# Delta rule: the 8-wide diagonal blocks of a triangular inverse solved on VectorE, in place of two levels of products on TensorE

## The chip, the cores and the metric

The kernel runs on one core of a Trainium2 chip. The metric is device time in microseconds (us). "Before" was timed three times, and its profile is of one further execution.

## The reference

One decoder layer over 256 tokens of width 2048: an input projection, two token mixers (a gated delta rule and a differential softmax attention), a gated merge, an output projection with a layer norm, and a SwiGLU feed-forward with a layer norm. The part that matters is the delta rule, for 16 heads in chunks of 64 tokens:

```
a_mat = where(strict, einsum(k_beta, k) * decay, 0)          # 64 x 64, strictly lower triangular
u, w  = triangular_solve(a_mat + eye(64), [v * beta, k_beta * exp(g)])
then, chunk after chunk:  v_new = u - w S ;  o = q_dec S + qk v_new ;  S = S * g_tot + k_tail^T v_new
```

All of it is float32.

## The kernel before

**Large products.** Every weight matrix is cut into tiles of 256 rows by 512 columns. SP loads a tile into one of four buffers of `raw`; ScalarE rounds it into `whi` (L836, by `split`), VectorE subtracts to get the rest `wlo` (L1416, by `split`), and TensorE multiplies with both, 12 matmuls a tile (`gemm_tile`, L477, all recorded at L458). `split(n, s)` in slot s prepares tile s + 3. A body is 32 tiles, so it has 32 slots; in each slot every engine does its share of the tile and then the small work that the slot is given. The order is written by hand: each engine runs its own stream, and semaphores join them.

**The delta rule between the tiles.** Four heads and their four chunks of 64 are handled in each of the first four bodies (NB = 4); body 0 has a stream of its own, on VectorE and ScalarE bodies 1 to 3 are one loop. `dn_build(j, s)` builds the inverse of `a_mat + eye` in slots 13 to 27. Each 64 x 64 matrix is first treated as two diagonal blocks of 32, which lie as 8 groups of 32 columns on 128 partitions (128 x 256 elements in all). Slot 15 on VectorE makes the masked blocks `WT` (four operations, one for each 32 partitions) and the starting inverse `TT` for blocks of 2. Then five levels, slots 17 to 21 (`GROW`): TensorE multiplies (32 matmuls of 32 x 32 blocks; L595, recorded at L458, `B<-Pm,Pc`), and VectorE subtracts from PSUM, transposes and masks, and so hands `Pc` to the next level (L1601 to L1613). The first and the last level have 32 columns, the three between have 64. Slots 22 and 23 (`OFF_P`, `OFF_T`) make the 32 x 32 block off the diagonal, ScalarE copies the results in slot 24, and slots 25 and 26 make the part that joins the two halves of the 64-blocks.

On TensorE the products of a slot stand behind the tile of that slot, and wait for the semaphore `dve_x` (`dve_t`, `dve_p` in the later slots; `act_tt` for ScalarE's copies). On VectorE the operations of a slot stand behind its `split`, and most wait for the one before them by a counter (`ch`).

**Other work in the same slots.** VectorE: `MASK` (slots 17, 18) masks `decm`; `O_LO` (19, 20) splits an output of the body before; the convolution (`CONV_SLOTS`, L1560) has six passes in each of slots 22, 23, 29 and 30 and a transpose in 21 and 28. ScalarE: `silu(j, 1)` stands behind its copies in slot 24.

Of the kernel before, what the change touches and what calls it, by code (L numbers as in the profile page):

```python
# [18 lines left out]
ALU = mybir.AluOpType  # L19
# [3 lines left out]
P = 128  # L23
# [7 lines left out]
CH = 64  # L31
# [10 lines left out]
PV_SLOTS = [10, 15, 20, 25]  # L42
OH_SLOTS = [14, 19, 24, 29]
OA_SLOT, OA_HI, OA_LO, OA_LAST = 0, 8, 11, 29
CONV_LINKS, BUILD_LINKS, SCAN_LINKS, DA_LINKS = 12, 20, 7, 25
OT_SLOTS = (12, 14)
O_SCALED, O_BLOCKS, V_BLOCKS = 11, 12, 25
O_HI, O_LO = 18, (19, 20)
MASK = (17, 18)
SCAN = 1  # L50
TURN = range(1, 7)
# [4 lines left out]
DECAY = range(5, 9)  # L56
WARM = 2
LATE_LO = 4
GROW = {17: 0, 18: 1, 19: 2, 20: 3, 21: 4}
GROWN = len(GROW)  # L60
OFF_P, OFF_T = 22, 23
TPG = KC // TK
RING = 4
AHEAD = 3
# [39 lines left out]
def build(nc, xT, xrow, weights, w_ab, consts, early, params, lam_in, ln_in, out):  # L104
# [8 lines left out]
    with ctx:  # L113
# [81 lines left out]
        B8 = [b[:, :].rearrange("p (h d) -> p h d", h=8) for b in B]  # L195
        C8 = [b[:, 0:8 * SB].rearrange("p (h d) -> p h d", h=8) for b in B]
        TT, WT = Pm[:, :, 0:SB], Pm[:, :, SB:CH]

        def conv_in(kind, h):

# [86 lines left out]
        def end_at(s):  # L287
# [28 lines left out]
            dve_lnT dve_x1 pe_x1T x1f act_x1T dve_x1T pe_y act_beta act_gc pe_gT act_gT act_var dve_var act_root act_sig act_xn pro_chain ln_chain""".split()  # L316

        counted = """pe_conv dve_raw dve_conv act_silu dve_cw act_tap
            dve_g act_past act_decay pe_ktok act_sqk dve_ktail pe_kk dve_at dve_t act_tt dve_x pe_x pe_p dve_p pe_t
            pe_p21 act_p21 pe_x21 act_x21 dve_vS dve_v pe_kq dve_qk  # L320
            pe_z dve_vn pe_so act_s act_o0 pe_ks dve_r pe_o1 dve_o1 pe_qtok act_osq act_sqq
            dve_oh dve_oS pe_oT act_oT dve_oT
# [133 lines left out]
        def _(pe):  # L456
# [112 lines left out]
            def dn_build(j, s):  # L569

                if s == 13:
                    pe.wait_ge(N["act_silu"], 1 + 3 * j + 1)
                    pe.wait_ge(N["dve_conv"], 1 + 6 * j + 2)
                    pe.wait_ge(N["act_sqq"], 1 + j)
                    for t in range(TOK):
                        for h in range(HB):
                            last = nc.tensor.transpose(B4[3 - 2 * t][:, h, :], cT[:, 0, h, t * P:(t + 1) * P], ident)  # L577
                    last.then_inc(N["pe_ktok"], 1)
                if s == 14:
                    pe.wait_ge(N["act_sqk"], 1 + 2 * j + 2)  # L580
                    pe.wait_ge(N["dve_ktail"], 1 + j + 1)
                    for t in range(TOK):
                        for h in range(HB):
                            kc = cT[:, 0, h, t * P:(t + 1) * P]
                            last = mm(B4[2 + t][:, h, :], kc, kc)
                    last.then_inc(N["pe_kk"], 1)
                if s in GROW:
                    k = GROW[s]
                    f0, f1 = SB if k == 0 else 0, SB if k == GROWN - 1 else CH
                    pe.wait_ge(N["dve_x"], 1 + GROWN * j + k + 1)  # L590
                    waits_end()
                    for i in range(8):
                        for q in range(4):
                            a = sub(q)
                            last = mm(B8[1][a, i, f0:f1], Pc[a, i, :], Pm[a, i, f0:f1])  # L595
                    last.then_inc(N["pe_x"], 1)
                if s == OFF_P:
                    pe.wait_ge(N["dve_t"], 1 + 2 * j + 1)
                    waits_end()
                    for i in range(8):  # L600
                        for q in (0, 2):
                            last = mm(C8[2][sub(q + 1), i, :], AT[sub(q), i, sub(q + 1)], Tc[sub(q), i, :])
                    last.then_inc(N["pe_p"], 1)
                if s == OFF_T:
                    pe.wait_ge(N["dve_p"], 1 + j + 1)
                    waits_end()
                    for i in range(8):
                        for q in (0, 2):
                            b = sub(q + 1)
                            last = mm(C8[1][sub(q), i, :], Pc[b, i, :], TT[b, i, :])  # L610
                    last.then_inc(N["pe_t"], 1)
                if s == 25:
                    pe.wait_ge(N["dve_t"], 1 + 2 * (j + 1))
                    pe.wait_ge(N["act_tt"], 1 + j + 1)
                    waits_end()
                    for i in range(HB):
                        mm(B8[1][CH:P, i, :], AT[0:CH, i, CH:P], T[0:CH, i, :])
                        last = mm(B8[1][0:CH, HB + i, :], AT[0:CH, HB + i, CH:P], T[0:CH, HB + i, :])
                    last.then_inc(N["pe_p21"], 1)
                if s == 26:  # L620
                    pe.wait_ge(N["act_p21"], 1 + j + 1)
                    waits_end()
                    for i in range(HB):
                        mm(B8[2][0:CH, i, :], Pm[CH:P, i, :], TTf[CH:P, i, CH:P])
                        last = mm(B8[1][0:CH, i, :], Pm[0:CH, HB + i, :], Pm[0:CH, i, :])
                    last.then_inc(N["pe_x21"], 1)
# [207 lines left out]
        def _(act):  # L834
# [157 lines left out]
            def dn_build(j, s):  # L992
# [17 lines left out]
                if s == 14 and isinstance(j, int):  # L1010
                    decay(j)
                if s == 24:
                    act.wait_ge(N["dve_t"], 1 + 2 * j + 1)
                    for q in range(4):
                        a = slice(q * SB, (q + 1) * SB)
# [2 lines left out]
                        a = slice(q * SB, (q + 1) * SB)  # L1018
                        last = copy(T[a, :, a], Tc[a])
                    last.then_inc(N["act_tt"], 1)  # L1020
                    silu(j, 1)
                if s == 25:
                    act.wait_ge(N["dve_t"], 1 + 2 * (j + 1))
                    act.wait_ge(N["act_tt"], 1 + j + 1)
                    copy(Pm[0:CH, 0:HB, :], TTf[CH:P, HB:8, CH:P])
                    act.wait_ge(N["pe_p21"], 1 + j + 1)
                    copy(Pm[CH:P, 0:HB, :], B8[1][CH:P, 0:HB, :])
                    copy(Pm[0:CH, HB:8, :], B8[1][0:CH, HB:8, :]).then_inc(N["act_p21"], 1)
                if s == 26:
                    act.wait_ge(N["pe_x21"], 1 + j + 1)  # L1030
                    copy(TTf[0:CH, 0:HB, CH:P], B8[2][0:CH, 0:HB, :], -1.0)
                    copy(TTf[0:CH, HB:8, CH:P], B8[1][0:CH, 0:HB, :], -1.0).then_inc(N["act_x21"], 1)
# [379 lines left out]
        def _(dve):  # L1412
# [56 lines left out]
            def prologue(s):  # L1469
# [9 lines left out]
                if s == 11:  # L1479
                    m0, e0, i0 = (CONST[n][0] for n in ("pairs", "eye", "incl"))  # L1480
                    levels = cst[:, m0:m0 + 6 * CH].rearrange("p (m c) -> p m c", c=CH)
                    for q in range(4):
                        a, f = slice(q * SB, (q + 1) * SB), q % 2 * SB
                        V.tensor_copy(masks[a, 0, :], levels[a, 0, f:f + SB])
                        V.tensor_copy(masks[a, 2:6, :], levels[a, 2:6, f:f + SB])
                        V.tensor_copy(masks[a, 6, :], cst[a, e0 + f:e0 + f + SB])
                        tt(masks[a, 1, :], cst[a, i0 + f:i0 + f + SB], cst[a, e0 + f:e0 + f + SB], ALU.subtract)
                if s == 4:
                    a0 = CONST["negdist"][0]
                    pro(ts(c("same"), cst[:, a0:a0 + P], -1e9, ALU.is_ge))  # L1490
# [80 lines left out]
            def dn_build(j, s, ch):  # L1571
# [16 lines left out]
                if s == 15:  # L1588
# [6 lines left out]
                        a = slice(q * SB, (q + 1) * SB)  # L1595
                        last = tt(WT[a], AT[a, :, a], rep(masks[:, 1, :], 8)[a], ALU.mult)
                    ch(last)
                    ch(tt(Tc[:, :, :], WT, rep(masks[:, 0, :], 8), ALU.mult))
                    V.transpose(flat(Pc[:, :, :]), flat(Tc[:, :, :])).then_inc(N["dve_x"], 1)
                    ch(tt(TT, rep(masks[:, 6, :], 8), Tc[:, :, :], ALU.subtract))  # L1600
                if s in GROW:  # L1601
                    k = GROW[s]
                    dve.wait_ge(N["pe_x"], 1 + GROWN * j + k + 1)
# [2 lines left out]
                        V.transpose(Tc[:, :, :], TT).then_inc(N["dve_t"], 1)  # L1606
                    else:
                        if k == 0:
                            ch(tt(WT, WT, B8[1][:, :, SB:CH], ALU.subtract))
                        else:  # L1610
                            ch(tt(Pm[:, :, :], Pm[:, :, :], B8[1], ALU.subtract))
                        ch(V.transpose(Tc[:, :, :], WT))
                        tt(Pc[:, :, :], Tc[:, :, :], rep(masks[:, k + 2, :], 8), ALU.mult).then_inc(N["dve_x"], 1)  # L1613
                if s in MASK:
                    i = MASK.index(s)
                    ch(tt(decm[:, 4 * i:4 * i + 4, :], decm[:, 4 * i:4 * i + 4, :], rep(c("same"), 4), ALU.mult))
# [589 lines left out]
```

## Time and profile before

| | |
|---|---|
| median of 3 timed runs | 1911.3 us (1910.58 to 1912.15) |
| profiled execution | 1913.78 us |
| its span | 1911.9 us |
| mean granted clock of TensorE | 0.998 of full speed |
| busy, TensorE (matmul) / VectorE / ScalarE | 99% / 69% / 48% of the span |

The span is from the first to the last instruction of the profiled execution; what lies around it is 1.9 us. The profiled execution is 2.5 us above the median of the timed runs. A busy TensorE says here that matmuls follow each other without a gap, and the work between the tiles is part of that.

### The profile page before, as it was taken

What the parts mean: (1) busy time and instruction counts of PE and PEld (TensorE: products, weight loads), DVE (VectorE), ACT (ScalarE), POOL (GpSimd) and SP (SyncE); (2) the same over time, 40 slices, a digit from 0 to 9 for tenths busy, and PEclk for the clock granted to TensorE, in tenths of its full rate; (3) what the DMA queues carried; (4) which work ended last, traced back from release to release, by engine and by line L of the source; (5) the groups of instructions that cost most, each with busy time, mean ns of one, the idle gap of its engine ahead of it and who ended that gap; (6) DMA issues with size and microseconds to landing.
All of it is one profiled execution on the core that took longest, in us unless ns stands there. A gap on an engine that the chain in (4) does not pass through costs nothing.

```text
span 1911.9 us, 31044 instructions
## 1 busy us (share of the span) xinstructions
PE 1896.8 (99%) x10215; PEld 1562.9 (82%) x10215; DVE 1318.8 (69%) x1829; ACT 919.0 (48%) x1270; POOL 189.8 (10%) x424
## 2 busy tenths in 40 slices
PE   9999999999999999999999999999999999999997
PEld 7888887878888888888888887888888888888886
DVE  7869788787766667676577657676774466654657
ACT  5655565554455555456444436444443444433442
POOL 0202021020014151414000000000000000000000
PEclk9999999999999999999999999999999999999999
DMA  7666657475667676766665675555655556555555
GB/s 271 190 208 199 210 188 210 164 222 166 199 202 229 223 236 214 245 212 201 217 195 187 223 252 189 177 195 188 198 194 192 195 190 195 193 195 192 193 189 175
DMA packets 115094, 387.68 MB, mean 203 GB/s; under 512 B 14192, under 2 KB 21168, under 8 KB 114864
## 3 DMA queue, kind: packets, MB, share of 16 engines
q1 hardware_dynamic: 97904, 351.65, 56.0%
q10 hardware_dynamic: 11712, 22.04, 3.7%
q0 software_dynamic: 5376, 12.59, 2.4%
q8 instruction: 68, 1.11, 0.2%
q14 instruction: 34, 0.28, 0.1%
HBM read 367.86 MB, written 18.37 MB: 202 GB/s over the span
## 4 chain that ended last, share of the span: by engine, by line
PE 98%; DVE 1%; issue 0%; ACT 0%; DMA 0%; DVEq 0%; SPq 0%; ACTq 0%
PE pg L458 92%; PE B L458 5%; DVE gates L1424 1%; DMA raw<-in_weights 0%; PE B L558 0%; PE B L577 0%; PE B L671 0%; ACT whi L836 0%; PE B L782 0%; DVE wlo L1416 0%; DVE act_b L1416 0%; PE B L710 0%; DVE lnst L2087 0%; DVE sm L1424 0%; DVE lnst L2092 0%
## 5 line engine op out<-in xcount | busy, mean ns | idle before, releaser
L1416 DVE TENSOR_TENSOR wlo<-raw,whi 128x1024 fp32r<-128x1024 f32 (+1 forms) x640 | 778.6, 1219 | 476.4 <-ACT whi L836 459.2
L836 ACT ACTIVATE whi<-raw 128x1024 fp32r<-128x1024 f32 (+1 forms) x640 | 674.1, 1057 | 766.4 <-PE pg L458 744.9
L458 PE MATMUL pg<-whi,act_x 128*128 128x512 f32 x2960 | 941.8, 394 | 0.6 <-ACT whi L836 0.6
L458 PEld LDWEIGHTS pg<-whi,act_x 128*128 128x128 f32 x2960 | 556.6, 188 | 125.1 <-issue 9.4
L458 PE MATMUL pg<-wlo,act_x 128*128 128x512 f32 x1480 | 574.9, 390 | 1.4 <-issue 1.4
L458 PE MATMUL pg<-whi,act_a 128*128 128x512 f32 x1632 | 504.9, 389 | 0.1
L458 PEld LDWEIGHTS pg<-whi,act_a 128*128 128x128 f32 x1632 | 306.3, 188 | 64.4 <-DVE act_a L1416 0.8
L458 PEld LDWEIGHTS pg<-wlo,act_x 128*128 128x128 f32 x1480 | 278.5, 188 | 54.7
L458 PE MATMUL pg<-wlo,act_a 128*128 128x512 f32 x816 | 317.5, 389 | 0.0
L458 PEld LDWEIGHTS pg<-wlo,act_a 128*128 128x128 f32 x816 | 153.2, 188 | 31.6
L458 PE MATMUL pg<-whi,act_b 128*128 128x512 f32 x512 | 158.4, 389 | 0.0
L458 PEld LDWEIGHTS pg<-whi,act_b 128*128 128x128 f32 x512 | 96.1, 188 | 19.9
L458 PE MATMUL pg<-wlo,act_b 128*128 128x512 f32 x256 | 99.6, 389 | 0.0
L1848 DVE STREAM_TRANSPOSE soft<-hraw 32x256 f32<-32x256 f32 x208 | 90.6, 436 | 3.8
L458 PEld LDWEIGHTS pg<-wlo,act_b 128*128 128x128 f32 x256 | 48.0, 188 | 10.0
L1424 DVE SCALAR_TENSOR_TENSOR cT<-vda,cw,cT 128x255 f32<-128x255 f32 (+2 forms) x96 | 42.0, 479 | 1.3
L1137 ACT ACTIVATE soft<-soft,sm 128x128 f32<-128x128 f32 (+1 forms) x64 | 28.4, 445 | 27.8 <-DVE sm L1420 27.7
L1364 POOL TENSOR_TENSOR half<-dsm 128x8 f32<-128x8 f32 x24 | 13.6, 566 | 257.6 <-DVE dsm L1421 256.3
L1424 DVE SCALAR_TENSOR_TENSOR soft<-cst,sm,B 128x384 f32<-128x384 f32 x32 | 18.2, 611 | 21.0 <-PE B L458 20.3
L1366 POOL TENSOR_SCALAR half<-half 128x2 f32<-128x2 f32 (+1 forms) x72 | 31.3, 435 | 6.3
L1375 POOL DMA_DIRECT2D gates<-turn_p x48 | 26.1, 550 | 37.3 <-DMA turn_p<-gates 37.3
L1375 POOL DMA_DIRECT2D qT<-turn_c x32 | 17.7, 560 | 114.2 <-DMA turn_c<-hraw 114.2
(251 smaller groups left out, 1089.2 us busy)
## 6 DMA issues: line engine op xcount, KB each, us to landing
raw<-in_weights SPq DMA_DIRECT2D x646, 512.0 KB, 4.2
turn_c<-hraw ACTq DMA_DIRECT2D x8, 512.0 KB, 3.6
qT<-turn_c POOLq DMA_DIRECT2D x32, 128.0 KB, 4.7
turn_q<-hraw ACTq DMA_DIRECT2D x6, 512.0 KB, 3.5
gates<-turn_q ACTq DMA_DIRECT2D x24, 128.0 KB, 4.4
turn_p<-gates POOLq DMA_DIRECT2D x12, 192.0 KB, 3.7
gates<-turn_p POOLq DMA_DIRECT2D x48, 48.0 KB, 3.7
decm<-sums_out ACTq DMA_DIRECT2D x4, 512.0 KB, 4.2
```

The source lines that it names most:

```text
L458: return nc.tensor.matmul(o, l, r, start=start, stop=stop)
L836: return nc.scalar.activation(o, i, ACT.Copy, scale=scale)
L1137: last = nc.scalar.activation(pr[:, m, a:b], pr[:, m, a:b], ACT.Exp, bias=sm[:, 28 + i:29 + i], accum_out=sm[:, 32 + i:33 + i])
L1364: ch(G.tensor_tensor(a, o, o, ALU.mult))
L1366: ch(G.tensor_scalar(a, a, -0.5, 1.5, ALU.mult, ALU.add))
L1375: pool.dma_start(dst[b * SB:(b + 1) * SB], scratch[:, :, b].rearrange("a x (q i) -> x a q i", i=SB)).then_inc(full, 16)
L1416: return V.tensor_tensor(o, a, b, op)
L1424: return V.scalar_tensor_tensor(out=o, in0=a, scalar=s, in1=b, op0=op0, op1=op1)
L1848: ins = V.transpose(blocks_out(turned)[b * SB:(b + 1) * SB, :, :, a, :], blocks_in[a * SB:(a + 1) * SB, :, :, b, :])
```

## The change

The two smallest block sizes above 2 are left out of the levels: `GROW` has three entries, in slots 20 to 22. The inverses of the 8 x 8 diagonal blocks now come from forward substitution on VectorE. Slot 16 transposes `WT` with its columns rearranged, multiplies by a selection mask `sel`, adds up, and so lays one 8 x 8 block on each partition (`a8`, 64 elements), beside an identity `t8`. Seven steps follow, each of two operations on `[128, n, k+1]` elements (7 to 16 of them): `u8 = column * row`, `t8 = t8 - u8`. One step is in slot 16, three each in slots 17 and 18. Slot 19 spreads `t8` out again, and two transposes give `TT` and `Tc`, with which the first of the remaining products starts. `OFF_P`, `OFF_T` and the slots of the 64-blocks come one slot later, ScalarE's copies move from slot 24 into 25, behind `silu`, and `O_LO` moves to slots 26 and 27.

```diff
-CONV_LINKS, BUILD_LINKS, SCAN_LINKS, DA_LINKS = 12, 20, 7, 25
+CONV_LINKS, BUILD_LINKS, SCAN_LINKS, DA_LINKS = 12, 33, 7, 25
-O_HI, O_LO = 18, (19, 20)
+O_HI, O_LO = 18, (26, 27)
-GROW = {17: 0, 18: 1, 19: 2, 20: 3, 21: 4}
+GROW = {20: 0, 21: 1, 22: 2}
-OFF_P, OFF_T = 22, 23
+OFF_P, OFF_T, OFF_COPY, OFF_64 = 23, 24, 25, 26
+EB = 8
+SOLVE = {16: range(0, 1), 17: range(1, 4), 18: range(4, 7)}
...
+        sel = masks[:, 0, 0:SB // EB]
+        eye8 = masks[:, 2:4, :].rearrange("p m c -> p (m c)")
+        a8, t8, u8 = (Tc[:, 2 * i:2 * i + 2, :].rearrange("p m c -> p (m c)").rearrange("p (r c) -> p r c", c=EB) for i in range(3))
+        def rows_apart(rows):
+            return rows.rearrange("p i (b g) -> p g i b", g=EB)
+        def blocks_apart(buf):
+            return buf[:, :, :].rearrange("p g (b x) -> p g b x", x=EB)
+        def below(k):
+            n = EB - 1 - k
+            return [ap.broadcast_to([P, n, k + 1]) for ap in (a8[:, k + 1:EB, k:k + 1], t8[:, k:k + 1, 0:k + 1])] + [
+                u8[:, 0:n, 0:k + 1], t8[:, k + 1:EB, 0:k + 1]]
...
# TensorE, dn_build
-                            last = mm(B8[1][a, i, f0:f1], Pc[a, i, :], Pm[a, i, f0:f1])
+                            last = mm(B8[1][a, i, f0:f1], (Tc if k == 0 else Pc)[a, i, :], Pm[a, i, f0:f1])
-                if s == 25:
+                if s == OFF_64:
-                if s == 26:
+                if s == OFF_64 + 1:
...
# ScalarE, dn_build
                 if s == 24:
+                    silu(j, 1)
+                if s == OFF_COPY:
                     act.wait_ge(N["dve_t"], 1 + 2 * j + 1)
...
-                    silu(j, 1)
-                if s == 25:
+                if s == OFF_64:
-                if s == 26:
+                if s == OFF_64 + 1:
...
# VectorE, prologue, slot 11
-                        V.tensor_copy(masks[a, 0, :], levels[a, 0, f:f + SB])
-                        V.tensor_copy(masks[a, 2:6, :], levels[a, 2:6, f:f + SB])
-                        V.tensor_copy(masks[a, 6, :], cst[a, e0 + f:e0 + f + SB])
+                        V.tensor_copy(masks[a, 4:6, :], levels[a, 4:6, f:f + SB])
+                    V.tensor_reduce(sel, ident.rearrange("p (m b) -> p b m", b=SB // EB), X, ALU.add)
+                    pro(V.memset(eye8, 0.0))
+                    pro(V.memset(eye8[:, 0:EB * EB:EB + 1], 1.0))
...
# VectorE, dn_build: slot 15 ends with the first line's wait
                     ch(last)
-                    ch(tt(Tc[:, :, :], WT, rep(masks[:, 0, :], 8), ALU.mult))
-                    V.transpose(flat(Pc[:, :, :]), flat(Tc[:, :, :])).then_inc(N["dve_x"], 1)
-                    ch(tt(TT, rep(masks[:, 6, :], 8), Tc[:, :, :], ALU.subtract))
+                if s == 16:
+                    ch(V.transpose(Tc[:, :, :], rows_apart(WT)))
+                    ch(tt(blocks_apart(Pc), blocks_apart(Tc), sel.unsqueeze(1).unsqueeze(3).broadcast_to([P, EB, SB // EB, EB]), ALU.mult))
+                    V.tensor_reduce(a8, Pc[:, :, :].rearrange("p g (b x) -> p g x b", x=EB), X, ALU.add)
+                    ch(V.tensor_copy(t8, eye8.rearrange("p (r c) -> p r c", c=EB)))
+                if s in SOLVE:
+                    for k in SOLVE[s]:
+                        col, row, part, rest = below(k)
+                        ch(tt(part, col, row, ALU.mult))
+                        ch(tt(rest, rest, part, ALU.subtract))
+                if s == 19:
+                    ch(tt(blocks_apart(Pc), t8.unsqueeze(2).broadcast_to([P, EB, SB // EB, EB]),
+                          sel.unsqueeze(1).unsqueeze(3).broadcast_to([P, EB, SB // EB, EB]), ALU.mult))
+                    ch(V.transpose(rows_apart(TT), Pc[:, :, :]))
+                    V.transpose(Tc[:, :, :], TT).then_inc(N["dve_x"], 1)
                 if s in GROW:
...
-                            ch(tt(WT, WT, B8[1][:, :, SB:CH], ALU.subtract))
+                            ch(V.tensor_copy(WT, B8[1][:, :, SB:CH]))
...
-                        tt(Pc[:, :, :], Tc[:, :, :], rep(masks[:, k + 2, :], 8), ALU.mult).then_inc(N["dve_x"], 1)
+                        tt(Pc[:, :, :], Tc[:, :, :], rep(masks[:, k + 4, :], 8), ALU.mult).then_inc(N["dve_x"], 1)
```

On TensorE, in the loop of bodies, this stood before from the end of slot 17 to the end of slot 19. `pg` are the two tiles' accumulators, `B` the PSUM bank of the products, and a row with `x31` is the rest of 32 matmuls.

```order
L458 MATMUL B<-Pm,Pc 32x32 [waits dve_x]
L458 MATMUL B<-Pm,Pc 32x32 x31
L458 MATMUL pg<-whi,act_x 128x512 [waits lo_done,hi_done]
...
L458 MATMUL B<-Pm,Pc 32x64 [waits dve_x]
L458 MATMUL B<-Pm,Pc 32x64 x31
L458 MATMUL pg<-whi,act_x 128x512 [waits lo_done,hi_done]
```

Now three tiles run without anything between them, and the first product, behind the tile of slot 20, takes `Tc`:

```order
L477 MATMUL pg<-whi,act_x 128x512
L477 MATMUL pg<-whi,act_x 128x512 [waits lo_done,hi_done]
L477 MATMUL pg<-wlo,act_x 128x512
...
L477 MATMUL pg<-whi,act_x 128x512
L477 MATMUL B<-Pm,Tc 32x32 [waits dve_x]
L477 MATMUL B<-Pm,Tc 32x32 x31
L477 MATMUL pg<-whi,act_x 128x512 [waits lo_done,hi_done]
```

The first wait for `dve_x` of a body has moved from behind the tile of slot 17 to behind that of slot 20, and two of the products with 64 columns are gone.

On VectorE, in the same loop, this stood before from the end of slot 15 to the update of slot 17; `split` is the row with `wlo`, and a REGISTER_ALU works out the count that a wait is for.

```order
L1416 TENSOR_TENSOR Pm<-AT,masks 32x8x32 x3
L339 REGISTER_ALU
L1416 TENSOR_TENSOR Tc<-Pm,masks 128x256 [waits build_chain]
L339 REGISTER_ALU
L1599 STREAM_TRANSPOSE Pc<-Tc 128x256 [waits build_chain]
L1416 TENSOR_TENSOR Pm<-masks,Tc 128x8x32
L339 REGISTER_ALU
L1435 REGISTER_ALU [waits build_chain]
L1416 TENSOR_TENSOR wlo<-raw,whi 128x1024 [waits tile_used,hi_done]
```

Now slot 16 reads, from the end of slot 15 on:

```order
L1436 TENSOR_TENSOR Pm<-AT,masks 32x8x32 x3
L358 REGISTER_ALU
L1455 REGISTER_ALU [waits build_chain]
L1436 TENSOR_TENSOR wlo<-raw,whi 128x1024 [waits tile_used,hi_done]
L1620 STREAM_TRANSPOSE Tc<-Pm 128x256
...
L1436 TENSOR_TENSOR Pc<-Tc,masks 128x256 [waits build_chain]
...
L1622 TENSOR_REDUCE Tc<-Pc 128x64 [waits build_chain]
L1623 COPY Tc<-masks 128x64
...
L1436 TENSOR_TENSOR Tc<-Tc 128x7 [waits build_chain]
```

The three operations that led to the first product have gone from slot 15, and behind the `split` of slot 16 there stands the laying out of the blocks.

Of slots 18 and 19 VectorE's stream now has this (the steps of three to five rows are shown, the `split` of slot 19, and the end):

```order
L1436 TENSOR_TENSOR Tc<-Tc 128x3x5 [waits build_chain]
...
L1436 TENSOR_TENSOR Tc<-Tc 128x7 [waits build_chain]
...
L1436 TENSOR_TENSOR decm<-decm,cst 128x512 [waits build_chain]
...
L1436 TENSOR_TENSOR wlo<-raw,whi 128x1024 [waits tile_used,hi_done]
L1436 TENSOR_TENSOR Pc<-Tc,masks 128x256
...
L1632 STREAM_TRANSPOSE Pm<-Pc 128x8x8x4 [waits build_chain]
...
L1633 STREAM_TRANSPOSE Tc<-Pm 128x256 [waits build_chain]
```

The last row is the one that raises `dve_x`, and everything in slots 16 to 19 stands ahead of it on the same engine.

## Rows read from the trace of the kernel before

**Rows 1.** Page, part 1 (busy) and part 4 (chain that ended last)

```profile
PE 1896.8 (99%) x10215; PEld 1562.9 (82%) x10215; DVE 1318.8 (69%) x1829; ACT 919.0 (48%) x1270; POOL 189.8 (10%) x424
...
PE 98%; DVE 1%; issue 0%; ACT 0%; DMA 0%; DVEq 0%; SPq 0%; ACTq 0%
```

**Rows 2.** Timeline, TensorE, body 1: start us, duration us, operation, records

```profile
171.97 0.62 PE L458 MATMUL pg<-whi,act_x 128*128 128x512 f32 x2
...
174.69 0.39 PE L458 MATMUL pg<-whi,act_x 128*128 128x512 f32 x1
175.00 0.75 PE L458 MATMUL B<-Pm,Pc 32*32 32x32 f32 x64
...
178.63 1.10 PE L458 MATMUL B<-Pm,Pc 32*32 32x64 f32 x64
...
190.59 0.75 PE L458 MATMUL B<-Pm,Pc 32*32 32x32 f32 x64
```

**Rows 3.** Timeline, VectorE, body 1, slots 15 to 17; in brackets idle time ahead

```profile
170.57 1.71 DVE L1416 TENSOR_TENSOR Pm<-AT,masks 32x256 f32<-32x256 f32 x4
...
173.71 2.36 DVE L1416 TENSOR_TENSOR wlo<-raw,whi 128x1024 fp32r<-128x1024 f32 x2 [0.19 <-DVE Pm L1416]
175.99 0.41 DVE L1416 TENSOR_TENSOR Pm<-Pm,B 128x256 f32<-128x256 f32 x1
176.44 0.45 DVE L1612 STREAM_TRANSPOSE Tc<-Pm 128x256 f32<-128x256 f32 x1
176.91 0.42 DVE L1416 TENSOR_TENSOR Pc<-Tc,masks 128x256 f32<-128x256 f32 x1
177.26 0.68 DVE L1416 TENSOR_TENSOR decm<-decm,cst 128x512 f32<-128x512 f32 x1
```

**Rows 4.** Timeline, VectorE, body 1, two small operations that wait for each other

```profile
147.50 0.17 DVE L1421 TENSOR_SCALAR dsm<-dsm 128x8 f32<-128x8 f32 x1
147.71 0.17 DVE L1424 SCALAR_TENSOR_TENSOR dsm<-dsm 128x8 f32<-128x8 f32 x1
```

**Rows 5.** Groups by form, VectorE, first 440 us: busy us, mean ns, idle ahead

```profile
L1688 DVE TENSOR_REDUCE dsm<-QKT 128x8 f32<-128x1024 f32 x3 | 3.7, 1221 | 0.1
...
L1541 DVE COPY cw<-par 128x48 f32 x3 | 0.6, 188 | 0.8 <-DVE zs L1416 0.8
```

**Rows 6.** Timeline, VectorE and TensorE, body 0, slots 15 to 17

```profile
62.92 1.71 DVE L1416 TENSOR_TENSOR Pm<-AT,masks 32x256 f32<-32x256 f32 x4
...
65.91 2.36 DVE L1416 TENSOR_TENSOR wlo<-raw,whi 128x1024 fp32r<-128x1024 f32 x2
...
66.29 0.75 PE L458 MATMUL B<-Pm,Pc 32*32 32x32 f32 x64
```

**Rows 7.** Timeline, VectorE and TensorE, body 3, slots 15 to 17

```profile
389.60 1.71 DVE L1416 TENSOR_TENSOR Pm<-AT,masks 32x256 f32<-32x256 f32 x4
...
394.04 0.75 PE L458 MATMUL B<-Pm,Pc 32*32 32x32 f32 x64
```

**Rows 8.** Timeline, VectorE, ScalarE and TensorE, body 1, slots 21 to 25

```profile
191.39 0.42 DVE L1416 TENSOR_TENSOR Pm<-Pm,B 128x256 f32<-128x256 f32 x1 [0.86 <-PE B L458]
...
194.96 0.42 DVE L1619 COPY Pc<-B 128x256 f32<-128x256 f32 x1 [0.44 <-PE B L458]
...
199.04 0.84 DVE L1420 TENSOR_SCALAR TTf<-B 32x256 f32<-32x256 f32 x2
...
200.39 2.70 DVE L1424 SCALAR_TENSOR_TENSOR cT<-vda,cw,cT 128x255 f32<-128x255 f32 x6
...
200.58 1.68 ACT L836 ACTIVATE TTf<-Pm 32x256 f32<-32x256 f32 x4
...
203.14 1.06 ACT L975 ACTIVATE cT<-cT 128x1024 f32<-128x1024 f32 x1
...
205.18 0.42 ACT L836 ACTIVATE Pm<-TTf 64x256 f32<-64x256 f32 x1
...
204.07 0.68 PE L458 MATMUL B<-T,AT 64*64 64x64 f32 x16
```

More of the change, by code:

```diff
@@ L318, in build @@
         counted = """pe_conv dve_raw dve_conv act_silu dve_cw act_tap
-            dve_g act_past act_decay pe_ktok act_sqk dve_ktail pe_kk dve_at dve_t act_tt dve_x pe_x pe_p dve_p pe_t
+            dve_g act_past act_decay pe_ktok act_sqk dve_ktail pe_kk dve_at dve_t act_tt dve_a8 pool_t8 dve_x pe_x pe_p dve_p pe_t
             pe_p21 act_p21 pe_x21 act_x21 dve_vS dve_v pe_kq dve_qk
```

## The prediction

> **What bounds the kernel now.** The first view is the page. TensorE is busy for 1896.8 us of 1911.9, and the chain that ended last is TensorE for 98% of its length, VectorE for 1% [rows 1]. The share of 69% for VectorE says nothing about one stage, so the second view is the timeline of a body. Within a run of plain tiles two rows that stand four pairs apart, one tile, are 174.69 - 171.97 = 2.72 us apart. With a product of 32 columns behind it, a tile takes 178.63 - 175.00 = 3.63 us; with one of 64 columns, (190.59 - 178.63) / 3 = 3.99 us [rows 2]. So the products are not hidden: each level stretches its slot by its own length, 0.91 or 1.27 us. The third view is VectorE's timeline at the same place. It ends the masked blocks at 170.57 + 1.71 = 172.28 and has the first `dve_x` done well before TensorE is ready for the first product at 175.00 [rows 2, 3]. In the levels VectorE is the one that waits, 0.86 us ahead of the last update [rows 8]. VectorE is off the path there with a cover of 2.7 us or less, and that is what the change spends.
>
> **What is removed.** Two levels of 64 columns in each of four bodies: 8 x 1.27 = 10.1 us of TensorE's path [rows 2]. The levels that stay have the same forms as before (32, 64 and 32 columns).
>
> **What is added on the path.** The new chain on VectorE runs from the end of slot 15 to `dve_x` at the end of slot 19. I price it for body 1, one row for each step.
>
> - *Each slot's start.* When a chained operation is ahead of a `split` in the loop, 0.19 us are idle, and a `split` takes 2.28 / 2 = 1.14 us until the next operation starts [rows 3]. Together 1.33 us, in slots 16, 17, 18 and 19.
> - *Slot 16, laying out.* A transpose of 256 elements holds up the one that waits for it by 176.91 - 176.44 = 0.47 us, an operation of that size by 0.45 us, and lets one that doesn't wait start after 177.26 - 176.91 = 0.35 us [rows 3]. The sum over groups of four has no row of its own size. A reduction of 1024 elements takes 1.22 us, as long as other VectorE work of that size [rows 5], so I take 0.35 us for 256. The copy of 64 elements is priced by one of 48, 0.19 us [rows 5], with 0.03 for the wait. That is 0.47 + 0.45 + 0.35 + 0.22 = 1.49 us.
> - *The steps.* 14 operations of 7 to 16 elements, each waiting for the one before. Two such operations of 8 elements start 147.71 - 147.50 = 0.21 us apart, of which 0.17 is the operation [rows 4]. So a step is 0.42 us: one in slot 16, three (1.26 us) in slots 17 and 18 each.
> - *Masks.* They stay in slots 17 and 18, 0.68 us each [rows 3].
> - *Slot 19.* Spread 0.45, transpose 0.47, transpose 0.45 to its end: 1.37 us [rows 3].
>
> Slot 16 takes 1.33 + 1.49 + 0.42 = 3.24, slots 17 and 18 each 1.33 + 1.26 + 0.68 = 3.27, slot 19 1.33 + 1.37 = 2.70. The sum is 12.48 us, and `dve_x` rises at 172.28 + 12.48 = 184.76. Between the engines I allow 0.05 us, the gap between the end of a product at 190.59 + 0.75 and the update that waits for it at 191.39 [rows 2, 8]. TensorE runs three plain tiles in the meantime and is ready at 175.00 + 3 x 2.72 = 183.16. **It waits 1.65 us behind the tile of slot 20.** Body 3 gives the same: 389.60 + 1.71 + 12.48 + 0.05 = 403.84 against 394.04 + 8.16 = 402.20 [rows 7]. I take 1.65 for bodies 1 to 3.
>
> In body 0 the masked blocks end at 64.63, only 1.66 us ahead of the product at 66.29, and no idle time is named ahead of the `split` there [rows 6]. With 0.05 in place of 0.19 in four slots the chain takes 11.92, so TensorE can start at 76.60 and was ready at 74.45: 2.15 us. The waits together are 3 x 1.65 + 2.15 = 7.1 us.
>
> **What is late next.** Behind the wait the levels run at the pace of rows 2, since VectorE needs 1.14 for the `split` and some 1.6 for update, transpose and mask of a level, 2.8 of the 3.6 us or more that TensorE takes. The tiles themselves stay covered: the `split` of slot 19 is done at about 183.4, and its tile (22) is needed after 188. The next place is the 64-block's first product, behind the tile of slot 26, which waits for ScalarE's copies, now behind `silu` and that behind the convolution. Counted from the first product TensorE reaches it after 3.63 + 3.99 + (204.07 - 190.59) = 21.1 us [rows 2, 8]. On the other side the second product ends after 4.73. VectorE then has the stretch that lasted from 191.39 to 203.09 before, less 0.44 of waiting, less the back-transfer of 200.39 - 199.04 = 1.35, which now comes later, and with an update of 64 columns more (1.54): 11.45. `silu` and a rounding take 205.18 - 203.14 = 2.04, the copies 203.14 - 200.58 = 2.56 [rows 8]. That is 20.9 with the gaps: 0.2 us to spare, so nothing is added, but each further 0.1 us there would cost 0.4 over the four bodies. `O_LO` (two operations of 512 elements, which start some 0.6 us apart from the next) goes from two slots of the levels to slots 26 and 27, which have neither levels nor convolution; I cost it at nothing, and at up to 1.2 us a body of VectorE's time, 3.6 in all, if VectorE were late there. The prologue's masks are fewer operations than before, three slots ahead of the chain; nothing too.
>
> **The sum.** -10.1 + 7.1 = -3.0 us. Against the profiled execution that is 1913.8 - 3.0 = 1910.8; that execution lies 2.5 us above the median of the three, so by the median 1911.3 - 3.0 = **1908.3 us**. About 0.2% (3.8 us) is what a measurement of this kernel can tell from no change, so this is "the same", 0.8 us short of "faster".
>
> **Bounds of what no row shows.** *Small operations:* from below 0.17 us, the operation without any gap [rows 4], which makes the waits 14 x 0.04 x 4 = 2.2 us shorter: 1906.1; from above 0.24, a gap twice as long, 1.7 us more: 1910.0. I stay with 0.21, which is the same kind of operation under the same kind of wait. *Three passes whose elements don't lie side by side* (the transpose that reads `WT` eight columns apart, the sum, the transpose that writes `TT` in that way): no row has such a pattern. From below they cost what the rows above say. From above I take the step from 256 to 512 elements, 0.68 - 0.42 = 0.26 us each [rows 3]: 0.8 a body, 3.2 us in all: 1911.5. I take the lower end, since it is the row of the same instruction and size, and keep the other in the range.
>
> **Rivals.** *VectorE is in time.* TensorE finds `dve_x` up, the full 10.1 us are kept, 1901.2 us. For it speaks that the cover of three plain tiles is 8.16 us and the new arithmetic itself is small (14 operations on at most 16 elements). Against it, the four `split`s and two masks alone take 4 x 1.33 + 2 x 0.68 = 6.7 of the 10.9 us that there are. The Trainium skill, VectorE: DVE Perf Modes, section "The TRN2 errata", gives a table by which an operation on SBUF costs 58 cycles plus one for each element, at 0.96 GHz; by that, an estimate, a step's operation would take about 0.08 us, the waits would nearly vanish and the time would be about 1901.5. Rows 4 have 0.17 for 8 elements and 0.21 with the wait, so the trace decides against it (the page says itself that its table comes out low). Less is needed for "faster" alone: the waits would have to sum to 6.3 us or less, 0.2 us a body below my sum.
>
> *The scattered passes are dear, and it gets slower.* The place is slots 16 and 19. If each of the three passes cost as much as one of 1024 elements, 1.22 in place of 0.42 us [rows 5], a body would wait 2.4 us longer: +9.6, 1917.9 us. It decides from waits that sum to 13.9 us (10.1 + 3.8), 1.7 us more a body than I have, or 0.57 more for each pass. The Trainium skill, Advanced Engine Details and Errata, section "Memory Cachelines", says that SBUF has lines of 16 bytes, and that accesses which go to another line each time pay a penalty, without its size; no row of before shows such a pattern on VectorE. Against a large penalty I have only that a transpose costs no more than an operation of its size that moves nothing across (0.45 and 0.42 us), and a sum no more than a subtraction of its size (1.22 and 1.14 to the next) [rows 3, 5].
>
> *The wait moves on.* TensorE meets the wait of slot 26 as well, for `act_tt`. At 0.5 us a body it adds 2.0: 1910.3, still the same.
>
> **How the numbers follow.** The wait as summed, with the scattered passes at anything up to twice their price, and with or without the wait in slot 26: 0.58, times from 1907.5 to 1913.5. Waits shorter by 0.2 to 1 us a body: 0.22, 1904 to 1907.5. No wait: 0.06, 1901.2. Scattered passes dear, or another wait of that size: 0.14, from 1915.1 up. So faster 0.28, same 0.58, slower 0.14. The range from 1904.0 to 1914.0 leaves out the third and the fourth case.
>
> **What would show it.** In the profile after: plain tiles of 2.72 us through slots 18 to 20; TensorE idle ahead of `B<-Pm,Tc`, released by VectorE, about 1.65 us in bodies 1 to 3 and 2.15 in body 0; two levels of 64 columns fewer, the others at 3.63 and 3.99 us; small operations 0.21 us apart; transposes of 0.45 us in slots 16 and 19. The prediction is wrong where that idle time is missing, where it is above 3 us, or where TensorE waits in a place that is not named here.

## The result and the profile after

| | before | after |
|---|---|---|
| median of 20 timed runs each | 1911.92 us (1909.87 to 1914.54) | 1915.40 us (1911.52 to 1919.68) |
| profiled execution, span | 1911.9 us | 1915.1 us |
| mean granted clock of TensorE | 0.998 | 0.995 |

The ratio is 1.0017 [1.0011, 1.0023]: after is 3.5 us slower, where 3.0 us faster was forecast, and 1915.4 lies above the range of 1904 to 1914.

The page of after answers to [rows 1], busy time by engine and the chain that ended last:

```profile
PE 1890.9 (99%) x9703; PEld 1558.6 (81%) x9703; DVE 1323.9 (69%) x1872; ACT 919.3 (48%) x1270; POOL 189.8 (10%) x424
...
PE 95%; DVE 3%; issue 1%; ACT 1%; DMA 0%; SPq 0%; ACTq 0%; DVEq 0%
```

TensorE's busy time has fallen by 5.9 us although levels of 10.1 us are gone, and VectorE is now 3% of the chain. The list of waits of TensorE (total us, times, longest) says where:

```profile
PE B L477 <- DVE Tc L1633: 9.6, 4, 2.9
```

One place, four times, and it is the place that was forecast: the first product, which waits for the last transpose of slot 19. But it is 9.6 us and not 7.1. The timeline of TensorE round the first two products of each body answers to [rows 2, 6, 7]; in brackets is the idle time ahead:

```profile
76.78 1.08 PE L477 MATMUL B<-Pm,Tc 32*32 32x32 f32 x64 [2.86 <-DVE Tc L1633]
...
78.38 0.63 PE L477 MATMUL pg<-wlo,act_x 128*128 128x512 f32 x1
78.81 1.05 PE L477 MATMUL pg<-whi,act_x 128*128 128x512 f32 x2
...
83.10 1.09 PE L477 MATMUL B<-Pm,Pc 32*32 32x64 f32 x64
...
187.97 0.74 PE L477 MATMUL B<-Pm,Tc 32*32 32x32 f32 x64 [2.24 <-DVE Tc L1633]
...
193.17 1.09 PE L477 MATMUL B<-Pm,Pc 32*32 32x64 f32 x64
...
298.06 1.08 PE L477 MATMUL B<-Pm,Tc 32*32 32x32 f32 x64 [2.25 <-DVE Tc L1633]
...
303.09 1.10 PE L477 MATMUL B<-Pm,Pc 32*32 32x64 f32 x64
...
407.98 0.74 PE L477 MATMUL B<-Pm,Tc 32*32 32x32 f32 x64 [2.24 <-DVE Tc L1633]
...
411.63 1.10 PE L477 MATMUL B<-Pm,Pc 32*32 32x64 f32 x64
```

Look at the distance from the first product to the second, 3.63 us in [rows 2]. In body 3 it is 411.63 - 407.98 = 3.65; in bodies 0 to 2 it is 6.32, 5.20 and 5.03. No idle time is named in there: matmuls of the same form start 78.81 - 78.38 = 0.43 us apart, where an undisturbed tile has 2.72 / 12 = 0.23 [rows 2]. The stretch is a loss of 2.69 + 1.57 + 1.40 + 0.02 = 5.7 us that the list of waits doesn't have. Windows of body 0 (length, busy time of the five engines, granted clock, share of the DMA engines, GB/s) say what it is:

```profile
66.00:73.75 7.75, 7.75 (x35) 6.21 (x34) 7.13 (x22) 3.05 (x3) 2.40 (x4) 1.00 0.80 214
73.75:76.78 3.03, 0.17 (x1) 0.03 (x1) 2.93 (x6) 1.06 (x1) 0.00 (x0) 0.89 0.51 183
76.78:79.50 2.72, 2.72 (x68) 2.37 (x69) 2.48 (x5) 0.00 (x0) 0.00 (x0) 0.50 0.60 193
79.50:83.10 3.60, 3.60 (x9) 2.38 (x8) 0.92 (x1) 0.00 (x0) 0.00 (x0) 0.52 0.73 246
83.10:90.71 7.61, 7.61 (x154) 5.93 (x153) 6.27 (x12) 3.71 (x6) 0.00 (x0) 1.00 0.20 57
```

The granted clock is full until TensorE runs out of work, falls during the idle time, stays at 0.50 (1.2 of 2.4 GHz) for the product and nearly the whole tile behind it, and is full again from the second product on. In body 1 the fall comes a little later: the granted clock is 1.00 through the wait and 0.65 from 187.97 to 190.50. The first product there takes 0.74 us, as long as at full clock, and it is the tile behind it that is slow.

VectorE's timeline in body 1 answers to [rows 3, 4]:

```profile
173.06 1.71 DVE L1436 TENSOR_TENSOR Pm<-AT,masks 32x256 f32<-32x256 f32 x4
...
176.13 0.64 DVE L1620 STREAM_TRANSPOSE Tc<-Pm 128x256 f32<-128x256 f32 x1
176.81 0.43 DVE L1436 TENSOR_TENSOR Pc<-Tc,masks 128x256 f32<-128x256 f32 x1
177.27 0.63 DVE L1622 TENSOR_REDUCE Tc<-Pc 128x64 f32<-128x256 f32 x1
177.83 0.18 DVE L1623 COPY Tc<-masks 128x64 f32<-128x64 f32 x1
...
179.76 1.21 DVE L1436 TENSOR_TENSOR Tc<-Tc 128x12 f32<-128x12 f32 x6
181.00 0.69 DVE L1436 TENSOR_TENSOR decm<-decm,cst 128x512 f32<-128x512 f32 x1
...
186.74 0.61 DVE L1632 STREAM_TRANSPOSE Pm<-Pc 128x256 f32<-128x256 f32 x1
187.38 0.45 DVE L1633 STREAM_TRANSPOSE Tc<-Pm 128x256 f32<-128x256 f32 x1
```

From the end of the masked blocks to the end of the last transpose it is 187.83 - 174.77 = 13.06 us; 12.48 was forecast. Three operations account for the difference: the transpose that reads eight columns apart (0.64), the sum over groups (0.63) and the transpose that writes eight columns apart (0.61). The other transpose, of the same size with its elements side by side, takes 0.45. Six small chained operations take (181.00 - 179.76) / 6 = 0.21 us each, as forecast.

So in this pair of profiles TensorE's path changed by -10.1 + 9.6 + 5.7 = +5.2 us. The spans differ by 3.2. The rest is in the execution of before: it has one idle stretch of 1.44 us in body 2 (below) that after lacks, and in after body 0 starts some 0.6 us earlier.

**The theories.** A: the loss has two parts, the longer wait (scattered passes), and the clock that falls behind it. Rivals: B, TensorE's slow stretch comes from something else that the change does at that time (VectorE's transposes or the loads, say), and not from the idle time ahead of it; C, the scattered passes alone would explain the miss, and with them at their forecast price the forecast sum would hold.

### The profile page after: what moved, and what is told of

Its sections match the earlier page's. It is cut to its first block, busy times and chain, and to the rows that moved or that the text cites. A ratio compares the mean times of both kernels' runs of the same rounds, so it can differ in the third digit from the quotient of the medians.

```text
span 1915.1 us, 30087 instructions
## 1 busy us (share of the span) xinstructions
PE 1890.9 (99%) x9703; PEld 1558.6 (81%) x9703; DVE 1323.9 (69%) x1872; ACT 919.3 (48%) x1270; POOL 189.8 (10%) x424
## 4 chain that ended last, share of the span: by engine, by line
PE 95%; DVE 3%; issue 1%; ACT 1%; DMA 0%; SPq 0%; ACTq 0%; DVEq 0%
PE pg L477 89%; PE B L477 5%; DVE gates L1444 1%; DVE Tc L1436 0%; DMA raw<-in_weights 0%; ACT whi L855 0%; DVE wlo L1436 0%; DVE decm L1436 0%; PE B L577 0%; PE B L690 0%; PE B L596 0%; ACT hraw L855 0%; DVE Pc L1436 0%; PE B L801 0%; DVE Pm L1632 0%
```

## The experiments

Each edit is against the kernel after. `e1` to `e4` ran on one chip beside before at 1911.56 us (22 runs), `e5` to `e8` on another beside before at 1912.91 us (16 runs). After was timed only for the result, beside before at 1911.92 us. A difference from after therefore goes across groups whose before differs by 0.4 or 1.0 us; where it matters, the difference of each kernel from its own before is given too.

**Filling the idle time (`e3_filler`).** TensorE gets eight more matmuls whose result nobody reads, ahead of the wait; VectorE's chain is as it was. They go to a bank that is free then.

```diff
+                    if k == 0:
+                        pe.wait_ge(N["dve_at"], 1 + j + 1)
+                        for _ in range(8):
+                            mm(B[3][:, :], act_x[:, 0, 0, 0:P], act_x[:, 0, 0:2, :].rearrange("p a b -> p (a b)"))
                     pe.wait_ge(N["dve_x"], 1 + GROWN * j + k + 1)
```

> The changed kernel with eight matmuls of 512 columns on TensorE (about 1.8 us, result unused) behind the tile of slot 20, ahead of the wait for dve_x. The wait ends at the same time, but TensorE is idle for only about 0.4 us of it in bodies 1 to 3 and 1.0 in body 0. Clock theory: the clock stays full, the product takes 0.75 us and the tile after it 2.85, and the time is before - 10.1 + 9.6 = before - 0.5 us, about 1911.4, 4 us below the changed kernel. Wait alone: as the changed kernel, 1915.4. Form of the product: 1915.4, with the product still slow.

Measured: 1911.31 us (1910.51 to 1911.92, 11 runs), ratio 0.9998 [0.9989, 1.0007]. TensorE in body 1:

```profile
183.00 1.97 PE L477 MATMUL B<-act_x 128*128 128x512 f32 x8
185.46 0.74 PE L477 MATMUL B<-Pm,Tc 32*32 32x32 f32 x64 [0.48 <-DVE Tc L1637]
...
189.09 1.10 PE L477 MATMUL B<-Pm,Pc 32*32 32x64 f32 x64
```

The product still starts as late as VectorE lets it, and TensorE does more work than in after, yet the kernel is 4.1 us faster (3.7 us when each is taken against its own before). The distance to the second product is 3.63 us again, and the granted clock of the whole run 0.998. VectorE's chain is as long as in after (13.1 us in body 1), and its transposes and the loads are those of after, so B falls: the slow stretch goes when the idle time goes. 1911.3 is also about what the removed levels and the waits alone give from the before of this group, 1911.56 - 10.1 + 9.6 = 1911.1.

**Scattered passes side by side (`e4_side_by_side`).** The two transposes and the sum read and write their elements side by side, with the same sizes. Another matrix comes out than the inverse; the order and number of operations is that of after.

```diff
-            return rows.rearrange("p i (b g) -> p g i b", g=EB)
+            return rows
...
-                    V.tensor_reduce(a8, Pc[:, :, :].rearrange("p g (b x) -> p g x b", x=EB), X, ALU.add)
+                    V.tensor_reduce(a8.rearrange("p r c -> p (r c)"), Pc[:, :, :].rearrange("p g (x b) -> p (g x) b", x=EB), X, ALU.add)
```

> The changed kernel with the three passes over scattered elements (two transposes, the sum over groups of four) reading and writing elements that lie side by side; the columns are not rearranged, so the inverse that comes out is another one. Scattered passes dear: each falls back to the 0.42 to 0.45 us of the rows of before, the chain is 0.6 us shorter, the waits are 1.65 and 2.3 us, 2.3 us less in all: 1913.1 if the clock falls as often as before, down to 1909 if it falls less often. If what I took for the pattern's price is the first use of data after another operation or the like, the passes stay at 0.6 us and the time at 1915.4.

Measured: 1911.50 us (1908.38 to 1913.97, 11 runs), ratio 0.9999 [0.999, 1.0008]. The three passes by form (busy us, mean ns):

```profile
L1632 DVE STREAM_TRANSPOSE Pm<-Pc 128x256 f32<-128x256 f32 x4 | 1.8, 446 | 0.1
...
L1620 DVE STREAM_TRANSPOSE Tc<-Pm 128x256 f32<-128x256 f32 x4 | 1.7, 437 | 0.0
L1622 DVE TENSOR_REDUCE Tc<-Pc 128x64 f32<-128x256 f32 x4 | 1.7, 420 | 0.1
```

That is the price I had taken, and the waits come out as I had summed them (2.15 and three times 1.65). TensorE's timeline:

```profile
76.37 0.74 PE L477 MATMUL B<-Pm,Tc 32*32 32x32 f32 x64 [2.09 <-DVE Tc L1633]
...
185.87 0.74 PE L477 MATMUL B<-Pm,Tc 32*32 32x32 f32 x64 [1.65 <-DVE Tc L1633]
...
191.08 1.10 PE L477 MATMUL B<-Pm,Pc 32*32 32x64 f32 x64
...
404.87 0.74 PE L477 MATMUL B<-Pm,Tc 32*32 32x32 f32 x64 [1.67 <-DVE Tc L1633]
...
408.53 1.09 PE L477 MATMUL B<-Pm,Pc 32*32 32x64 f32 x64
```

In bodies 0 to 2 the second product comes 5.2 us after the first, in body 3 3.66. Three times some 1.57 us are lost to the clock, as the windows of body 1 show (a granted clock of 0.70 and 0.64 between the two products):

```profile
183.00:185.87 2.87, 1.22 (x7) 0.71 (x5) 2.61 (x6) 1.06 (x1) 0.00 (x0) 1.00 0.69 204
185.87:188.50 2.63, 2.63 (x69) 2.20 (x70) 2.56 (x5) 0.00 (x0) 0.00 (x0) 0.70 0.58 212
188.50:191.08 2.58, 2.58 (x8) 1.77 (x6) 0.74 (x1) 0.00 (x0) 0.00 (x0) 0.64 0.67 225
```

So C falls too: with every VectorE price right, the forecast would still have been 3 us too low in the median. The timed runs of this kernel tell it a second way, since each has its own mean granted clock. The one run at 0.998 took 1908.38 us, the three at 0.997 1909.66 to 1910.73, the four at 0.995 or 0.996 that lie highest 1913.11 to 1913.97. 1908.3 was forecast.

**Both terms taken away (`e8_side_by_side_filler`).** The edits of the two before, with five extra matmuls, since the wait is shorter.

```diff
-            return rows.rearrange("p i (b g) -> p g i b", g=EB)
+            return rows
...
+                        for _ in range(5):
+                            mm(B[3][:, :], act_x[:, 0, 0, 0:P], act_x[:, 0, 0:2, :].rearrange("p a b -> p (a b)"))
```

> The changed kernel with the three passes on elements that lie side by side (the inverse that comes out is another one) and with five matmuls of 512 columns, about 1.15 us, on TensorE ahead of the wait for dve_x. Both things that the forecast did not have are taken away: the waits end as in the forecast, 7.1 us in all, and TensorE is idle for only 0.5 us (0.95 in body 0) of each. Clock theory: the clock stays full and the time is the forecast's own sum, before - 10.1 + 7.1, about 1908.7. Wait alone, or another cause that the filler does not touch: as the kernel with the passes side by side, 1911.5.

Measured: 1908.48 us (1907.89 to 1909.24, 11 runs), ratio 0.9976 [0.9967, 0.9985], clock 0.998 in every run. The second product follows 3.62 to 3.64 us behind the first in each body. In body 1:

```profile
184.29 0.74 PE L477 MATMUL B<-Pm,Tc 32*32 32x32 f32 x64 [0.53 <-DVE Tc L1637]
...
187.93 1.10 PE L477 MATMUL B<-Pm,Pc 32*32 32x64 f32 x64
```

With both missing terms out, the time is the forecast's own. Against its own before, which is 1.0 us above that of the result, the difference is -4.4 us where the sum has -3.0, so the sum is met to 1.4 us.

**The masks out of the chain (`e1_masks_late`).**

```diff
-MASK = (17, 18)
+MASK = (26, 27)
```

> The changed kernel with the two operations that mask decm moved from slots 17 and 18 to slots 26 and 27; nothing else. Clock theory (the loss is the wait for the first dve_x, 9.6 us in the profile, plus the granted clock that falls to half behind the idle time, 5.7 us there): the chain ahead of dve_x is shorter by 2 x 0.72 us, so TensorE waits 0.8 us in bodies 1 to 3 and 1.4 in body 0, 3.8 in all, the clock stays full, and the time is before - 10.1 + 3.8 = before - 6.3 us, about 1905.6. Rival, wait alone (the halved clock was a matter of that one profile): 5.8 us less than the changed kernel, about 1909.6. Rival, form of the product (the product that takes Tc is slow in itself): about 1909.6 too, with the product still at 1.08 us in some body.

Measured: 1905.29 us (1904.59 to 1905.88, 6 runs), ratio 0.9967 [0.9955, 0.9979]. TensorE in body 1 (in body 0 it waits 1.26 us):

```profile
182.81 0.74 PE L477 MATMUL B<-Pm,Tc 32*32 32x32 f32 x64 [0.82 <-DVE Tc L1633]
...
186.47 1.09 PE L477 MATMUL B<-Pm,Pc 32*32 32x64 f32 x64
```

The wait is shorter by 1.4 to 1.6 us, the two masks, and sums to 3.7 us. The clock stays full behind it (3.63 to 3.66 us to the second product). The 1.4 us of masks a body bring some 10 us: 10.1 between the medians, 9.8 when each kernel is taken against its own before. Of that, 9.6 - 3.7 = 5.9 us are waiting and some 4 are clock.

**The levels a slot later (`e2_levels_later`).** TensorE gets one more plain tile ahead of the first product.

```diff
-GROW = {20: 0, 21: 1, 22: 2}
+GROW = {21: 0, 22: 1, 23: 2}
...
-OFF_P, OFF_T, OFF_COPY, OFF_64 = 23, 24, 25, 26
+OFF_P, OFF_T, OFF_COPY, OFF_64 = 24, 25, 26, 27
```

> The changed kernel with the three levels and all that follows them (off-diagonal block, ScalarE's copies, 64-blocks) one slot later, so that four plain tiles cover the new chain in place of three. Clock theory: cover grows by 2.72 us, so no wait in bodies 1 to 3, 0.1 us in body 0, no fall of the clock, and the whole 10.1 us of the two levels are kept: about 1901.9. Wait alone: 9.6 us less than the changed kernel, about 1905.8. Form of the product: 1905.8 with slow products after full tiles. A wait may show later, behind the tile of slot 27, for ScalarE's copies; that would add to each.

Measured: 1904.49 us (1904.06 to 1904.79, 5 runs), ratio 0.9964 [0.9951, 0.9978]. The wait ahead of the first product is gone, but two new ones have come (TensorE's waits):

```profile
PE B L477 <- DVE Pc L1652: 1.6, 4, 0.4
...
PE B L477 <- DVE Tc L1639: 1.2, 4, 0.5
```

They are the products of slots 24 and 25, which now come right behind slots 22 and 23, where VectorE has the convolution, six passes and 2.7 us in each. 2.8 us of the 10.1 are given back there, and the time is 2.6 above the 1901.9 that I expected.

**Both moves (`e5_masks_late_levels_later`).** If the new waits come from the convolution alone they stay; if VectorE is late there because its solve ended late, they go.

```diff
-MASK = (17, 18)
+MASK = (26, 27)
...
-GROW = {20: 0, 21: 1, 22: 2}
+GROW = {21: 0, 22: 1, 23: 2}
...
-OFF_P, OFF_T, OFF_COPY, OFF_64 = 23, 24, 25, 26
+OFF_P, OFF_T, OFF_COPY, OFF_64 = 24, 25, 26, 27
```

> The changed kernel with the masks in slots 26 and 27 and the levels one slot later. With the levels later alone TensorE had no wait for the first product but 2.8 us in all in slots 24 and 25, ahead of the off-diagonal block. If those come from the convolution that now stands ahead of it on VectorE, taking the masks away changes nothing there, since VectorE was in time for the first product already: 1904.5 again. If they come from the chain of the solve that still runs late into the levels, they shrink by up to the 1.4 us a body that the masks take: 1902.

Measured: 1903.16 us (1902.89 to 1903.61, 4 runs), ratio 0.995 [0.9934, 0.9965]. Of the two waits only that for `Pc` L1652 is left, 1.2 us in all, 0.3 in each body. So both readings were half right. The wait of slot 24 came from the late solve: it is gone now that VectorE is early enough to wait for TensorE in the levels (0.51 and 0.37 us in body 1). That of slot 25 is put down to the convolution: in body 1 the copy that ends it starts at 198.63, behind the six passes of slot 23, which start at 194.92, and a `split`. The convolution itself was not moved.

**The end of the solve in slot 18 (`e7_end_in_18`).** The last three operations of the chain move one `split` forward.

```diff
-                if s == 19:
+                if s == 18:
                     ch(tt(blocks_apart(Pc), t8.unsqueeze(2).broadcast_to([P, EB, SB // EB, EB]),
```

> The changed kernel with the end of the solve in slot 18, ahead of the second mask and of the split of slot 19; the masks stay in 17 and 18. The chain ahead of dve_x is shorter by 1.33 + 0.72 us (1.19 + 0.72 in body 0): waits of 0.2 us in bodies 1 to 3 and 0.95 in body 0, 1.6 in all. Clock theory: no fall of the clock at idle times as short as these, time before - 10.1 + 1.6, about 1903.2. Wait alone: the changed kernel less 8.0, about 1907.4.

Measured: 1906.34 us (1905.92 to 1907.86, 6 runs), ratio 0.9968 [0.9956, 0.998]. The wait ahead of the first product shrank to the 1.7 us I expected, and the clock stayed full; but a second wait is there that I had not seen. TensorE's waits:

```profile
PE B L477 <- DVE Pc L1436: 2.6, 4, 0.7
PE B L477 <- DVE Tc L1633: 1.7, 4, 0.9
```

and VectorE's timeline in body 1, from the last transpose of the solve to the first update:

```profile
181.59 0.45 DVE L1633 STREAM_TRANSPOSE Tc<-Pm 128x256 f32<-128x256 f32 x1
181.96 0.65 DVE L1436 TENSOR_TENSOR decm<-decm,cst 128x512 f32<-128x512 f32 x1
182.80 2.36 DVE L1436 TENSOR_TENSOR wlo<-raw,whi 128x1024 fp32r<-128x1024 f32 x2 [0.19 <-DVE decm L1436]
185.08 0.42 DVE L1642 COPY Pm<-B 128x256 f32<-128x256 f32 x1
```

Between them stand the mask of slot 18, now behind the solve's end, and the `split`s of slots 19 and 20, so the update starts at 185.08 although its product began at 182.19. The waits sum to 4.3 us.

**The same, and the masks late (`e6_end_in_18_masks_late`).**

```diff
-MASK = (17, 18)
+MASK = (26, 27)
...
-                if s == 19:
+                if s == 18:
```

> The changed kernel with the masks of decm in slots 26 and 27 and with the spread and the two transposes that end the solve moved from slot 19 to the end of slot 18, ahead of the next tile's split. Clock theory: masks late left idle times of 0.8 us (bodies 1 to 3) and 1.26 us (body 0); the split of slot 19 (1.33 us, 1.19 in body 0) is no longer ahead of dve_x, so TensorE waits nowhere, or under 0.1 us in body 0, the clock stays full and all of the 10.1 us is kept: 1901.5. If the levels then find VectorE late (its split of slot 19 now stands between dve_x and the first update), a wait of up to 0.5 us a body comes back and it is 1903.5. Wait alone (no clock): the same, since no wait is left.

Measured: 1901.80 us (1901.39 to 1902.13, 5 runs), ratio 0.9943 [0.9929, 0.9956]. It leaves out nothing of the computation and beats both kernels. TensorE in body 1 has no idle time ahead of any product, and the second product follows 3.64 us behind the first, the third 3.98 behind the second (at 188.13), as in [rows 2]:

```profile
180.51 0.75 PE L477 MATMUL B<-Pm,Tc 32*32 32x32 f32 x64
...
184.15 1.10 PE L477 MATMUL B<-Pm,Pc 32*32 32x64 f32 x64
```

This is the rival "VectorE is in time" (1901.2 us), reached by moving five operations of a body, two masks and the three that end the solve. Against its own before it is 11.1 us faster, 1.0 more than the two levels. `e5`, `e7` and `e8` are also 0.8 to 1.4 us below the sums made from 1912.91; three of the 16 runs of before in that group had a clock of 0.997 and took 1914.15 to 1915.48. Whether idle stretches like the one of 1.44 us account for that was not tested.

## Why the prediction was wrong

- *What is removed:* right. With the waits taken away the full 10.1 us are there (`e6_end_in_18_masks_late`), and the levels that stay keep 3.63 and 3.99 us wherever the clock is full.
- *The place and the cause of the wait:* right. TensorE waits behind the tile of slot 20, for the last transpose of slot 19, with the four `split`s and the two masks in the chain. Taking the masks out shortened it by their own 1.4 to 1.6 us.
- *Small operations:* right, 0.21 us each. The 0.08 us on which a rival rested did not come about.
- *The three scattered passes:* mis-sized. I took the price of a pass with its elements side by side [rows 3, 5], and they take 0.2 us more each: from start to start 0.68, 0.56 and 0.64 us (176.81 - 176.13, 177.83 - 177.27, 187.38 - 186.74) in place of 0.47, 0.35 and 0.47. The chain is 13.06 us in place of 12.48, and the waits 9.6 in place of 7.1: +2.5 us. The upper bound of 0.26 each held it, and this alone would have ended at 1910.8, inside the range. The side-by-side kernel, with the waits as summed, shows that no other term of the chain was off.
- *What is late next:* this is the step that failed. It says that behind the wait the levels run at the pace of [rows 2]. The reason given there is VectorE's work alone. The levels do run at that pace from the second product on. Ahead of it the first product, or the tile behind it, runs at half the clock in three of the four bodies of the profile. That cost 5.7 us in this execution, which took 1916.98 us and so lies 1.6 above the median, and about 4 in the median (1915.40 - 1911.31 = 4.1 with the filler, 3.7 when each is taken against its own before). In the trace of before no product of the inverse waits, so no row there prices what comes behind a wait; but a wait was priced as the time waited and nothing else, and no bound was set for what comes behind it. None of the three rivals has it either.
- *The prologue, `O_LO`, the wait of slot 26:* right, they add nothing that shows. TensorE has no wait for `act_tt` in after.

The sum as measured: -10.1 + 9.6 + 4 = +3.5, and +3.5 us was the difference of the medians. The 4 is itself taken from medians, so what this tests is the rest of it: the kernel with the filler should lie 0.5 us below its own before, and lies 0.25 below.

Two hits are luck. By the line of 3.8 us that the prediction drew, +3.5 us still is "the same", to which it gave most weight; but that came of two terms that it did not have in its sum. And 1915.4 us lies where it put the scattered passes when they are dear, though the waits sum to 9.6 us and not to the 13.9 of that case. None of its three signs of being wrong appeared: the longest wait was 2.86 us, at the place that was named.

One stretch of before might have been a warning. At the start of the kernel, behind idle time, eight matmuls of a tile take 3.75 us, and the same eight of the next tile take 2.00:

```profile
5.83 3.75 PE L458 MATMUL pg<-whi,act_x 128*128 128x512 f32 x8 [0.57 <-ACT whi L836]
...
10.71 2.00 PE L458 MATMUL pg<-whi,act_x 128*128 128x512 f32 x8
```

Whether that was the clock stays open, since the windows view gives a granted clock of 1.00 for that stretch.

The wider spread of after goes with the clock. Of its 20 timed runs the three at a granted clock of 0.998 took 1911.73 to 1913.39 us, and the two at 0.994 1917.87 and 1919.68. With the filler all 11 runs have 0.998 and lie within 1.4 us.

## What to carry to other kernels

Where a change makes an engine wait that never waited before, price the wait and what the engine does behind it: here waits of 1.65 to 2.9 us on TensorE cost up to 2.7 us more in clock, and taking 1.4 us a body of VectorE's work out from ahead of them returned 10 us over four bodies. Work that nobody needs soon (the masks) doesn't belong in a chain that the bounding engine waits for, and a chain that ends a slot sooner must also have its first follower free, or the wait only moves one product on. A pass whose elements don't lie side by side has a price of its own: here 0.2 us each, near the upper bound of 0.26 that the prediction set aside, and not at the lower one that it took.

## What the runs showed of the hardware

**In these runs TensorE's clock fell at idle times of 1.65 to 2.86 us, and not each time.** The table has the idle time ahead of the first product (in `e7` also of the second), and what followed:

| kernel | idle ahead, us | clock behind it |
|---|---|---|
| e7, e3, e8 | 0.26 to 0.97 | full |
| e1 | 0.80 to 1.26 | full |
| before, body 2 | 1.44 | full |
| e4, bodies 1 and 2 | 1.65, 1.66 | half |
| e4, body 3 | 1.67 | full |
| e4, body 0 | 2.09 | half |
| after, bodies 1 and 2 | 2.24, 2.25 | half |
| after, body 3 | 2.24 | full |
| after, body 0 | 2.86 | half |

A fall cost 1.4 to 2.7 us. Idle times of the same length had different outcomes, so their length alone doesn't decide, and what else does was not tested. The one of before is of another kind, since the profile names nothing that TensorE waits for in it ("issue"). It cost no clock; its row, and the windows ahead of its end and behind:

```profile
294.30 0.39 PE L458 MATMUL pg<-wlo,act_x 128*128 128x512 f32 x1 [1.44 <-issue]
...
291.00:294.30 3.30, 1.87 (x67) 1.23 (x66) 3.23 (x6) 1.06 (x1) 0.00 (x0) 1.00 0.93 207
294.30:296.90 2.60, 2.60 (x11) 1.88 (x10) 1.74 (x3) 0.00 (x0) 0.00 (x0) 1.00 0.54 194
```

**Scattered elements on VectorE.** 256 elements that lie 32 bytes apart cost 0.64 (read by a transpose), 0.63 (read by a sum) and 0.61 us (written by a transpose), against 0.44, 0.42 and 0.45 side by side: some 0.2 us, or half as much again. The Trainium skill, Advanced Engine Details and Errata, section "Memory Cachelines", says that an access which goes to another line of SBUF each time pays a penalty; these rows agree with it and give its size for this one pattern; other distances were not tried.
